# Modulation weights streamed beside the first mixers' weights, and a 16-bit look-up in the expert selection

## What is computed

```
# block 1: x = x + merge(gla(h), sliding window attention(h)) @ w_out;  x = x + peer(rmsnorm(x))
h = rmsnorm(x, norm_mix_g); proj = h @ w_in        # 6672 columns: gq gk gv gr glr sq sk sv gate_a gate_b
# block 2, modulated by a vector c:
mod = silu(c) @ w_ada + b_ada                      # (1024) @ (1024 x 6144)
shift1, scale1, gate1, shift2, scale2, gate2 = split(mod, 6)
h = rms_norm(x, g_mix) * (1 + scale1) + shift1     # first use of mod
# peer(h): for each token and each of 8 heads
s1, s2 = scores against 128 + 128 keys; v1, i1 = top_k(s1, 16); v2, i2 = top_k(s2, 16)
best, pos = top_k(v1[:, None] + v2[None, :], 16)   # of 16 x 16 sums
expert = i1[pos // 16] * 128 + i2[pos % 16]        # 16384 experts
out = sum over picks of softmax(best) * gelu(h . u[expert]) * v[expert]
```

## Time and profile before

| | |
|---|---|
| median of 3 runs | 3658.6 us (3657.64 to 3669.47) |
| profiled execution, its own time | 3667.88 us |
| its span in the trace | 3666.1 us |
| mean granted PE clock | 0.966 |
| busy: PE, DVE, ACT, POOL | 93%, 72%, 38%, 22% of the span |
| mean DMA traffic | 233 GB/s |

### The profile page before, as it was taken

The page is one execution under the profiler, slowest core; times in us unless marked ns, Lnnn a source line. Parts: engine busy times, 40 slices in busy tenths (PEclk is TensorE's granted clock), DMA queues, the critical chain, the costliest instruction groups (busy, mean ns, idle before and its releaser), DMA issues.

```text
span 3666.1 us, 47405 instructions
## 1 busy us (share of the span) xinstructions
PE 3425.9 (93%) x19255; PEld 3030.1 (83%) x19255; DVE 2656.3 (72%) x4558; ACT 1408.2 (38%) x1890; POOL 824.5 (22%) x534
## 2 busy tenths in 40 slices
PE   6999998999999999999998889789988999999998
PEld 5968678899999999788887776778988899888887
DVE  3346544269878797788888487459898897788887
ACT  4324542232232565333333435433332466333333
POOL 0000000004343231243332000002443331233332
PEclk9999999999999999999999999889999999999999
DMA  3202123249988899899997120216887899999996
GB/s 127 81 24 81 46 86 110 81 160 322 321 285 309 288 331 331 341 352 363 357 360 262 52 70 6 98 63 217 292 277 262 284 334 325 351 368 365 352 364 236
DMA packets 373518, 855.62 MB, mean 233 GB/s; under 512 B 22514, under 2 KB 237346, under 8 KB 340147
## 3 DMA queue, kind: packets, MB, share of 16 engines
q1 hardware_dynamic: 299570, 584.12, 45.6%
q0 software_dynamic: 73728, 268.47, 20.3%
HBM read 746.58 MB, written 105.93 MB: 233 GB/s over the span
## 4 chain that ended last, share of the span: by engine, by line
PE 71%; DVE 18%; DMA 5%; ACT 4%; issue 1%; POOL 0%; SPq 0%; DVEq 0%; POOLq 0%; ACTq 0%
PE ps L292 40%; PE ps L1372 28%; DVE parts L275 4%; DVE scr L1600 3%; DMA scr<-in_w_ada 2%; PE ps L314 1%; DMA scr<-in_p_rows_u,cst 1%; DVE scr L1643 1%; DVE scr L1635 1%; ACT parts L267 1%; DVE scr L2161 1%; DMA hbuf<-scr 1%; DVE scr L2159 1%; ACT scr L1438 1%; DVE scr L1581 1%
## 5 line engine op out<-in xcount | busy, mean ns | idle before, releaser
L292 PE MATMUL ps<-ht_hi,parts 128*128 128x384 f32 (+1 forms) x5008 | 1391.1, 354 | 60.3 <-DVE parts L275 55.9
L292 PEld LDWEIGHTS ps<-ht_hi,parts 128*128 128x128 f32 x5008 | 938.8, 193 | 108.3 <-DVE parts L275 62.3
L275 DVE TENSOR_TENSOR parts<-ring,parts 128x2048 fp32r<-128x2048 f32 (+1 forms) x317 | 724.3, 2286 | 386.7 <-ACT parts L267 385.0
L267 ACT ACTIVATE parts<-ring 128x2048 fp32r<-128x2048 f32 (+1 forms) x317 | 606.3, 1913 | 827.7 <-PE ps L1372 675.8
L292 PE MATMUL ps<-ht_lo,parts 128*128 128x384 f32 (+1 forms) x2504 | 878.4, 351 | 0.0
L320 ACT ACTIVATE scr<-ps 128x384 f32<-128x384 f32 (+2 forms) x497 | 244.1, 504 | 1077.5 <-PE ps L292 996.9
L1726 POOL DMA_INDIRECT scr<-in_p_rows_u,cst x256 | 428.6, 1674 | 1013.0 <-DVE scr L1600 656.5
L1726 POOL DMA_INDIRECT scr<-in_peer_v,cst x256 | 376.2, 1470 | 754.9 <-DVE xres L1617 611.2
L1372 PE MATMUL ps<-parts,ht_hi 128*128 128x512 f32 x2304 | 530.8, 391 | 5.7 <-DVE ht_hi L1690 5.7
L1372 PE MATMUL ps<-parts,ht_lo 128*128 128x512 f32 x2304 | 528.9, 390 | 7.3 <-DVE ht_lo L1690 7.3
L1372 PEld LDWEIGHTS ps<-parts,ht_hi 128*128 128x128 f32 x2304 | 434.6, 189 | 96.8 <-DVE ht_hi L1690 6.3
(11 more groups left out here) (233 smaller groups left out, 2561.5 us busy)
## 6 DMA issues: line engine op xcount, KB each, us to landing
ring<-in_peer_u SPq DMA_DIRECT2D x128, 1024.0 KB
ring<-in_peer_v SPq DMA_DIRECT2D x128, 1024.0 KB
hbuf<-scr SPq DMA_DIRECT2D x128, 384.0 KB
gbuf<-scr SPq DMA_DIRECT2D x96, 512.0 KB
scr<-gbuf SPq DMA_DIRECT2D x64, 768.0 KB, 9.4
scr<-hbuf SPq DMA_DIRECT2D x64, 768.0 KB, 11.7
ring<-in_w_in SPq DMA_DIRECT2D x35, 1024.0 KB
scr<-in_w_ada SPq DMA_DIRECT2D x48, 512.0 KB
```

What stands on the lines that cost most here:

```text
L267: e.activation(halves(m)[0], slot_view(m)[:, 0:units[m][0]], ACT.Copy).then_inc(A.sem, A.up(("hi", m)))
L275: e.tensor_tensor(lo, slot_view(m)[:, 0:units[m][0]], hi.bitcast(F32), ALU.subtract).then_inc(V.sem, V.up(("lo", m), ("slot", m)))
L292: ins = e.matmul(ps, l, r, start=(i == 0), stop=(i == n - 1))
```

## The change

There are three parts.

1. **Modulation among the mixers.** w_ada is read as 24 raw units of 256 columns (`plan_beside`), one behind each unit of weights of gq to gr (10 of them), gb, wb, wo and the first three of p1q (14 of them), except behind gq 0, gr 3 and gb 0. DVE makes the weighted sum over the 8 row groups (`ada_sums`: 8 dependent instructions on 128 x 256), which frees the slot. PE adds over partitions with one fp32 matmul of 256 columns (`ada_pe`). Two additions and two stores put mod into HBM. All `mod_*` steps leave peer 1's up stage, and the gathers of peer 1 get five row buffers in place of four. `after(m)` skips the raw unit.
2. **Look-up of places.** Steps 11 to 14 compare and multiply in fp16, and three halving additions in fp16 and a last one to fp32 take the place of the reduction.
3. **The gates' product** of a spread step is one instruction of 2048 elements and not two of 1024; and the planner's costs are new.

```diff
+        def plan_beside(name, wt, a, count):
+
+            for k in range(count):
+                planned((name, k), NC * 256, wcols(wt, a + 256 * k, 256))
+                s = len(ada)
+                if (name, k) not in (("gq", 0), ("gr", 3), ("gb", 0)):
+                    planned(("ada", s), UNIT, wcols(flat2("w_ada_2"), 256 * s, 256), raw=True)
+                    ada.append(number["ada", s])
+
...
+        ada, FIRST = [], 10
         plan_cols("gl", w1, 3072, 1, 128)
-        plan_cols("gq", w1, 0, 2)
-        plan_cols("gk", w1, 512, 2)
-        plan_cols("gv", w1, 1024, 4)
...
-        plan_cols("gb", w1, 5648, 4)
-        plan_cols("wb", flat2("w_branch_b"), 0, 4)
-        plan_cols("wo", flat2("w_out"), 0, 4)
-        plan_cols("p1q", flat2("w_peer_q"), 0, 8)
+        plan_beside("gb", w1, 5648, 4)
+        plan_beside("wb", flat2("w_branch_b"), 0, 4)
+        plan_beside("wo", flat2("w_out"), 0, 4)
+        plan_beside("p1q", flat2("w_peer_q"), 0, 3)
+        for k in range(3, 8):
+            planned(("p1q", k), NC * 256, wcols(flat2("w_peer_q"), 256 * k, 256))
...
+        def after(m):
+
+            m += 1
+            return m + 1 if m in ada else m
...
+        def ada_sums(e, w, s):
+            m = U["ada", s]
+            acc = ada_acc[s % 2]
+            wv = cview(slot_view(m), 256)
+            w.wait_ge(*at_point("c_act"))
+            w.wait_ge(*at_point("landed", m))
+            if s >= 2:
+                w.wait_ge(*at_point("ada_read", s - 2))
+            for cc in range(NC):
+                if cc == 0:
+                    ins = e.tensor_scalar(acc, wv[:, cc, :], ct[:, cc:cc + 1], None, ALU.mult)
+                else:
+                    w.wait_ge(*V.now())
+                    ins = e.scalar_tensor_tensor(out=acc, in0=wv[:, cc, :], scalar=ct[:, cc:cc + 1], in1=acc,
+                                                 op0=ALU.mult, op1=ALU.add)
+                ins.then_inc(V.sem, V.up(*([("slot", m), ("ada_sum", s)] if cc == NC - 1 else [])))
+
+        def ada_pe(e, w, s):
+            part = int(s >= FIRST)
+            a, b = PARTS[part]
+            key = ("mods", part)
+            if s == a:
...
+            w.wait_ge(*at_point("ada_sum", s))
...
+            e.matmul(psum(key)[0:n, 0:256], c("pick")[:, 13 - (s - a):13 - (s - a) + n], ada_acc[s % 2], start=(s == a),
+                     stop=(s == b - 1), skip_group_check=True).then_inc(P.sem, P.up(("ada_read", s), *names))
...
+        def ada_dve(e, w, part):
+            n = PARTS[part][1] - PARTS[part][0]
...
+            e.tensor_tensor(md[0:n, :], psum(key)[0:n, 0:256], bd[0:n, :], ALU.add).then_inc(
+                V.sem, V.up(("free", key), ("mod_done", part)))
...
             for name, dst in (("gq", QT), ("gk", KT)):
                 for s in range(2):
-                    split_lo(e, w, U[name, s] + 1)
+                    split_lo(e, w, after(U[name, s]))
                     put_dve(e, w, (name, s, 1), dst[:, 2 * s + 1, :], psum((name, s, 1)), (name, "dve"))
+                    if (name, s) != ("gq", 0):
+                        ada_sums(e, w, s - 1 if name == "gq" else s + 1)
...
             for s in range(4):
-                split_lo(e, w, U["gv", s] + 1)
+                split_lo(e, w, after(U["gv", s]))
                 for blk in (1, 3):
                     put_dve(e, w, ("gv", s, blk), VV[:, blk, s * 256:(s + 1) * 256], psum(("gv", s, blk))[:, 0:256], ("gv_out",))
+                ada_sums(e, w, 3 + s)
...
             for s in range(4):
-                split_lo(e, w, U["gb", s] + 1)
+                split_lo(e, w, after(U["gb", s]))
+                if s:
+                    ada_sums(e, w, FIRST + s - 1)
...
-                split_lo(e, w, U["wb", s] + 1)
+                split_lo(e, w, after(U["wb", s]))
...
+                ada_sums(e, w, FIRST + 3 + s)
             for s in range(4):
-                split_lo(e, w, U["wo", s] + 1)
+                split_lo(e, w, after(U["wo", s]))
                 for blk in range(NB):
...
-                w.wait_ge(*at_point("mod_used", s - 2))
-            e.dma_start(mw[k], inp["w_ada_2"].rearrange("o (c p) n -> p (o c) n", p=128)[:, :, 128 * s:128 * s + 128]).then_inc(
-                dm_mw[k].sem, dm_mw[k].up(("ada", s), by=16))
...
-                names = [("ps", ("mods",))] if n == MOD_STEPS - 1 else []
-                matmuls(e, psum(("mods",))[:, n:n + 1], [(mw[n % 2][:, cc, :], ct[:, cc:cc + 1]) for cc in range(NC)],
-                        ("mod_used", n), *names)
...
+                ada_sums(e, w, FIRST + 7 + s)
...
-            costs = [3.0] * 5 + [2.0] + [1.6] * 5 + [5.4, 4.4, 2.4, 4.4, 8.0]
-            one_step, one_dot, early = 1.65, 1.4, 92
+            costs = [3.0] * 5 + [2.4] + [1.6] * 5 + [4.8, 3.1, 1.4, 3.1, 8.0]
+            one_step, one_dot, early = 1.45, 1.4, 92
...
+                if self.nq == 16:
+                    ada_store(e, w, 1)
...
-                        if b == 1 and self.nq == 16 and a <= MOD_STEPS + 4:
-                            mod_sp(e, w, a)
...
-                        if b == 1 and nq == 16 and a <= MOD_STEPS + 4:
-                            mod_pe(e, w, a)
...
+                    split_lo(e, w, after(U[tag + "q", s]))
                     put_dve(e, w, (tag, "qp", 2 * s + 1), self.QP[:, :, 2 * s + 1, :],
                             psum((tag, "qp", 2 * s + 1)).rearrange("p (b t) -> p b t", b=NB), (tag, "qp_out", 1))
+                    if nq == 16 and s < 3:
+                        ada_sums(e, w, FIRST + 11 + s)
+                    if nq == 16 and s == 3:
+                        ada_dve(e, w, 1)
...
-                    e.tensor_copy(self.F16, self.I16.rearrange("p g k -> p (g k)"))
+                    Iv = self.I16.rearrange("p (h s) k -> p s h k", s=2)
+                    for r in range(2):
+                        e.tensor_copy(self.F16[:, r], bc(Iv[:, r].unsqueeze(3), [128, 8, 16, 2]))
...
+                    if r == 0:
+                        w.wait_ge(*self.pt("iota4"))
...
-                    e.tensor_tensor(self.EQ, bc(self.HF[r].rearrange("p (h k) -> p h k", h=8).unsqueeze(3), [128, 8, 16, 16]),
-                                    bc(it16.unsqueeze(1).unsqueeze(1), [128, 8, 16, 16]), ALU.is_equal).then_inc(V.sem, V.up())
+                    e.tensor_tensor(self.EQ, bc(self.AB[r].unsqueeze(2), [128, 8, 16, 16]),
+                                    bc(self.iota_a.unsqueeze(1), [128, 8, 16, 16]), ALU.is_equal).then_inc(V.sem, V.up())
                 if i in (12, 14):
...
-                    Fv = self.F16.rearrange("p (h s k) -> p h s k", h=8, s=2)
...
-                    e.tensor_tensor(self.EQ, self.EQ, bc(Fv[:, :, r, :].unsqueeze(2), [128, 8, 16, 16]), ALU.mult).then_inc(
-                        V.sem, V.up())
+                    e.tensor_tensor(self.EQ.rearrange(pairs, d=2), self.EQ.rearrange(pairs, d=2),
+                                    bc(self.F16[:, r].rearrange("p h a d -> p (h a) d").unsqueeze(2), [128, 128, 8, 2]),
+                                    ALU.mult).then_inc(V.sem, V.up())
+                    for n in (8, 4, 2):
+                        w.wait_ge(*V.now())
+                        e.tensor_tensor(self.EQ[:, :, 0:n, :], self.EQ[:, :, 0:n, :], self.EQ[:, :, n:2 * n, :],
+                                        ALU.add).then_inc(V.sem, V.up())
...
-                    e.tensor_reduce(self.IX[r].rearrange("p (h k) -> p h k", h=8), self.EQ, AX.X, ALU.add).then_inc(
-                        V.sem, V.up())
+                    e.tensor_tensor(self.IX[r].rearrange("p (h k) -> p h k", h=8), self.EQ[:, :, 0, :], self.EQ[:, :, 1, :],
+                                    ALU.add).then_inc(V.sem, V.up())
...
+                e.tensor_scalar(self.AB[0].rearrange("p h k -> p (h k)"), A0, MAGIC, None, ALU.subtract).then_inc(V.sem, V.up())
...
-                e.tensor_tensor(OH.rearrange(pairs, d=2),
+                e.tensor_tensor(OH.rearrange("p r t (i d) -> p (r t) i d", d=2),
...
+                                bc(self.RT[:, i, :, :, :].rearrange("p r t d -> p (r t) d").unsqueeze(2), [128, 16, 64, 2]),
                                 ALU.is_equal).then_inc(V.sem, V.up())
                 w.wait_ge(*V.now())
-                for g in range(2):
-                    names = [(self.tag, "one_hot", i)] if g else []
...
+                e.tensor_tensor(GO.rearrange("p x t (i d) -> p x t i d", d=2),
+                                bc(OH[:, 1:2, :, :].rearrange("p x t (i d) -> p x t i d", d=2), [128, 2, 8, 64, 2]),
+                                bc(self.RG[:, i, :, :, :].unsqueeze(3), [128, 2, 8, 64, 2]), ALU.mult).then_inc(
+                                    V.sem, V.up((self.tag, "one_hot", i)))
```

More of the change, by code:

```diff
@@ L62, in const_table @@
     add("one", np.ones((128, 1)))
+    add("pick", np.eye(27)[13:14] * np.ones((128, 1)))
     return np.concatenate(cols, 1), at
@@ L139, in build @@
         dm_hl = [steps(f"h_landed{i}") for i in range(2)]
```

(66 more changed lines are left out.)

128 lines of the change are left out of this document (44 added, 84 removed).

## The result

The changed kernel takes 3728.7 us, median of 4 runs (3724.3 to 3729.9), against 3664.0 of the kernel before in 4 runs. The ratio is 1.0166, 95% interval 1.0147 to 1.0185: slower by 1.7%. The prediction said 3701, within 3645 to 3755, and slower with 0.80. The profiled execution took 3724.33 (span 3722.5) against 3667.88 (3666.1), 56.4 of span. Between the medians it is 64.6, since the profiled execution is the shortest of its four here and lies above the median before.

What follows compares the result with a forecast made beforehand. PE, busy 93% of 3666.1 us, was taken as the bound. Mixers lose 134 us and the up stages gain 92 (54 + 38), so + 42 on the median 3658.6 gives 3701 us, range 3645 to 3755.

Steps and rivals of the forecast that it cites:

- What bounds the kernel: Whole kernel: PE, busy 93% of 3666.1 us; only removing PE's work or adding a wait of PE counts.
- the loop: Mixers: each unit runs through sums 3.6, two loads 8.3, split 4.3: 16.2 us against PE's 10.9 or 11.6.
- The table of units: Early stages: delay each unit adds, such as gv 0 4.6, wb 2 and 3 10.9 each, wo 0 13.6; all 134 us.
- the pair: Mixers: two queued loads of 1 MB, w_ada and the next split unit, taking 8.3 us with start and landing.
- Modulation leaves the up stage: Peer 1's up stage: without modulation it falls to peer 2's length, 722 − 668 = 54 us gained.
- Look-up and product: Up stages: look-up 6.87 to 4.13 us, gates' product 0.16 less per spread step; 20 and 7.5 us per stage.
- of these 27 us I take 19: Each up stage: of 27 us of DVE time saved, 19 shorten the stage, 38 for both.
- the loads are hidden: Mixers, faster rival: the loop falls below 11.6 us and the loss is zero, 3567 us; chance 0.06.
- PE's floor: Both up stages, faster rival: all waits go and PE alone sets the time, 3615 us; chance 0.07.
- The fp16 look-up: Up stages, rival: the fp16 look-up gives nothing, as broadcast compares run at 2.29; 3739 us; chance 0.12.
- the last rival: Mixers: loads quicker than the pair at 80.66, at 6.8 the loop costs 103, 3670 us; chance 0.09.

Runs made afterwards that it cites:

- e1: The changed kernel with SP issuing the split unit's load ahead of the w_ada load that stood before it: 3614.8 us, ratio to before 0.9847.
- e4: The changed kernel with 4 of the 8 dependent instructions in each sum over w_ada left out (modulation wrong): 3673.3 us, one execution.
- e6: The changed kernel with the sums over w_ada right behind the low part in gv, wb and wo, SP's order kept: 3687.8 us, one execution.
- e3: The changed kernel with the look-up, two gates' products and planner's costs of before, so only modulation is moved: 3749.2 us, ratio 1.0215.
- e11: The changed kernel with e1's order, wo 3's sums after the norm, x's first store earlier, and spread step cost 1.65, not 1.45: 3576.6 us, one execution.

## Why the prediction was right, step by step

**What bounds the kernel, and the loop: right.** PE waits where SP's order makes the loads late, at + 136.5 for + 134. The mechanism is shown by e1 (its order alone gives back 114 us with all work in place), e4 (what the sums lose, a turn loses) and e6 (the merges are in it). The table of units shows that the sum is not luck either: most units are within 1 us of what was predicted, and the largest miss is 2.3 (gr 2). Inside a turn, though, one price was off, and small errors of the others hid it. The sums are 0.34 + 7 × 0.52 = 4.0 us and not 3.6. The 0.40 taken from the 16 of L653 is the time from one start to the next of instructions that don't wait for each other and overlap; each of them takes 0.477. In the sums one takes 0.485, and as each waits for the one before, the next starts after 0.52. So the dependence costs 0.12 an instruction and not 0.04. Against these 0.4 us stand 0.2 less for the copies of gv (0.6 and not 0.8) and 0.1 or 0.2 less for the pair: from the issue of w_ada to the landing of w_in it takes 103.84 + 7.81 − 103.43 = 8.2, and 8.1 in wb, and not 8.3.

**Modulation leaves the up stage: right.** − 54 taken, 52 found (e3). Peer 2's stage, from which the 54 was read, had five row buffers already and peer 1's four, so the 54 took that difference in as well.

**Look-up and product: the durations right, the size of what comes back off.** DVE lost 583.86 − 560.21 = 24 us in peer 2's stage and 26 in peer 1's, for 27. The step that failed is "of these 27 us I take 19": it came to 12.6 in peer 1's stage (e3's 669.3 against the mean of 656.7) and 10.7 in peer 2's (667.6, the mean of before and e3, against 656.9). With the old costs it was 15.7 and 18.1. So the waits were judged about right, and the new costs, which I had priced at nothing, take back 3 and 7 us (the 3 is within what executions differ by, the 7 is not). That DVE's time can't all come back is not shown, for e11, one execution, has 24 and 27 with another cost of a spread step. Where the DVE time goes in the changed kernel, by DVE's waits in peer 2's stage (2527.4 to 3186.7), and then in e11:

```profile
DVE parts L292 <- ACT parts L284: 44.9, 13, 15.7
DVE scr L1533 <- ACT scr L1459: 25.2, 3, 10.6
DVE scr L1656 <- DMA scr<-in_p_rows_u,cst: 14.8, 6, 4.9
DVE ht_hi L1742 <- ACT ht_hi L1499: 7.5, 1, 7.5
```

```profile
DVE parts L296 <- ACT parts L288: 36.8, 16, 8.3
DVE scr L1540 <- ACT scr L1464: 22.9, 3, 9.7
DVE scr L1663 <- DMA scr<-in_p_rows_u,cst: 10.8, 6, 4.4
...
DVE ht_hi L1749 <- ACT ht_hi L1504: 1.4, 1, 1.4
```

PE waits 41.0 us for the split there, where it had waited 43.3: nearly the same wait. The time that DVE saves it waits itself: for ACT at the turn (L1533), for gathered rows (L1656) and at the end for ht_hi. In the kernel before the four waits were 44.2, 19.5, 8.8 and 1.4.

**The rivals.** That the loads are hidden is false here, and nearly true once SP's order is changed. But e1 is at 3615 and not at that rival's 3567: 23 us of delay stay ahead of the first up, the up stages gave some 20 less than taken, the kernel before was at 3668 beside it and not at 3659, and the other stages were some 3 shorter. The up stages did not fall to PE's floor. The fp16 look-up does give its DVE time; L1568 and L1574 take 1.23 us. The pair was quicker than I took by 0.1 to 0.2 us, and not by 1.5 as in the last rival. By the fit of the Trainium skill, page "DMA: Bandwidth & Descriptors", section "Anatomy of one DMA — SWDGE (gpsimd) path", a pair would be 6.8 us, an estimate; the trace shows 8.1 to 8.2 for loads that SyncE issues. The advice of the same page of the Trainium skill in "Rules for kernel authors", to issue early, is what e1 follows, and it is worth 114 us.

**The whole.** + 136.5 − 65.5 − 8.6 − 6.0 = + 56.4 of span against + 42: the loss was 2.5 larger, the gain 18 smaller, and the down stages and block 2's mixers were some 2 us shorter each, which is no more than executions of one kernel differ by. That the time came out inside the range rests on the size of the loss; the gain was 18 of 92 too high.

## What to carry to other kernels

A cheap extra stream on idle engines is not free if its buffer is freed late and its load stands ahead of the main stream's in one queue: follow, for each load, what the wait ahead of it in its queue is, and add up that loop, not the engines' busy time. Then try the other order of the two loads first; here it turned 1.7% slower into 1.5% faster. Take the price of a chain from a chain: starts of independent instructions in a row lie closer together (0.40 us here) than one of them takes (0.477). Where a list is laid out by costs, new costs are a change of their own, and need a measurement of their own when an operation becomes cheaper.
